# The z projections of a hybrid decoder step as block products with seven multiplications, two heads prepared in each

## Chip, cores and metric

One Trainium2 chip, one NeuronCore of it. The metric is the device time of one execution in microseconds; where several runs are given, their median.

## What is computed

One inference step of one decoder layer in float32, for 256 new tokens of a prompt and 8 x 4 tokens of running sequences: 288 token columns in all. Cut to what matters here:

```python
h = rmsnorm(x, norm1_w)
proj = jnp.einsum('btd,de->bte', h, w_in)      # 1024 -> pool 512, qkv 3072, a/b 16, z 1024, gates 2048
u_pool, u_qkv, b_raw, a_raw, z, gate_pool, gate_delta = jnp.split(proj, SPLITS, axis=-1)
y_pool, pool_buf_new = pool_mix(u_pool, pool_buf, ...)      # window means 2, 4, 8, 16, then w_pool
qkv, conv_buf_new = causal_conv(u_qkv, conv_buf, w_conv)    # width 4, then silu
o, s_new = gated_delta_chunked(l2norm(q), l2norm(k), v, g, beta, s0, chunk)   # 8 heads of 128
o = rmsnorm(o, o_norm_w) * jax.nn.silu(z)
merged = sigmoid(gate_pool) * (y_pool @ w_branch_pool) + sigmoid(gate_delta) * (o @ w_branch_delta)
x = x + merged @ w_out
x = x + hier_moe(rmsnorm(x, norm2_w), ...)     # 32 experts, top 2; gate, up, down
```

## The kernel before, in words

Each engine has its own program, written out by hand in order, and they meet at semaphores. There is no scheduler. The instructions of one engine run strictly in the order in which they stand.

**Projections.** `PROJ` lists 52 chunks of 128 output channels: 0 to 23 are q, k, v; 24 to 27 the pool groups; 28 to 35 z, a head each; 36 to 51 the gates. Two neighbouring chunks share one weight item of 1 MB (item 14 holds chunks 28 and 29). SyncE loads the items in order into slots of the arena (`SLOT_OF`), each when the item that held the slot has been read. Between the loads it issues the other transfers at fixed item numbers: `CONV_AT` and `ROWS_AT` (18), `CONV_AT + 1` (pool rows), `CONV_AT + 2` and `+ 3` (`load_states`), item 21 (a block of zeros from `X` to `x_image`), `DIAG_AT` (24).

**Two ways to multiply.** `proj(n)` makes one chunk with 8 matmuls of 288 columns. `fast_pair(i)` makes both chunks of an item by Strassen's scheme in Winograd's form: 7 block products P1, P6, P5, P7, P2, P3, P4 of 4 matmuls of 144 columns each. For it GpSimd makes four sums of weight blocks (`sum_weights`: four additions of 128 x 512) into slot 4 or 5. ScalarE copies P1 and P2 out of PSUM, and VectorE makes five additions of 144 columns (`add_u2`, `add_u4`, `add_u7`, `add_u5`, `add_u6`). P3 waits for `add_u4`, P4 for `add_u7`. Before, `FAST` holds items 1 to 11 (q, k, v) only.

**The stage of the change.** After q, k, v come the four pool chunks. VectorE makes the window sums of each group (`window(g)`, L2547 to L2558), TensorE then the four `pool_mix` products (L1564). Two z chunks are made among these (`Z_AHEAD`). After that comes a loop over the eight heads: `proj` of one more chunk, then `prep(h)` on TensorE (two products of keys with keys and queries, L1594). On VectorE `prep(h)` adds the decay rows to a mask (L2576), waits for ScalarE's three exponentials (`rows_exp`, L1067, L1070), multiplies (L2580) and scales the products (L2584, L2587). Between the heads stand small steps for the sample tokens (`sample_rows`, `sample_tiles`, `sample_flips`), and after head 4 `state_products(0)` (L1630). This one waits for `zb`, which GpSimd raises by `own_columns(0)` (L837), and `own_columns(0)` waits for the block of zeros to be in `x_image`. The decay rows of the heads go a round trip through DRAM (`head_rows`: out at L534, back to all partitions at L538). z itself leaves PSUM by a Silu on ScalarE (L975), one per chunk.

**Further on.** Gate chunks, the inversion of the 16 x 16 blocks (`diagonal_blocks` on SyncE, started when all eight heads are prepared), the scan over the chunks, the branches, `w_out`, and then the experts, whose weights (3 MB for each of 32) are streamed from DRAM.

The lines that bring the stage's order about:

```python
for n in range(Z_AHEAD):
    proj(N_Z + n)
    pool_mix(2 * n)
    pool_mix(2 * n + 1)
...
for h in range(H):
    proj(N_Z + Z_AHEAD + h)
    prep(h)
...
```

Of the kernel before, what the change touches and what calls it, by code (L numbers as in the profile page):

```python
# [21 lines left out]
H = 8  # L22
# [32 lines left out]
FAST = range(1, NQKV // 2)  # L55
# [4 lines left out]
SLOT_OF = [i % 4 if i < NQKV // 2 else i % RA for i in range(A_ITEMS)]  # L60
# [6 lines left out]
def sums_slot(i):  # L67
    return 4 + i % 2
# [21 lines left out]
Z_AHEAD = 2  # L90
# [12 lines left out]
MIX_BANK = (7, 4)  # L103
CONV_AT = NQKV // 2 + RA
ROWS_AT = NQKV // 2 + RA
DIAG_AT = (N_GATE + 2) // 2 + RA - 1
# [24 lines left out]
def hybrid_step(nc, x_prompt, x_sample, cache_pool, cache_conv, state_delta, norm1_w, w_in, w_pool,  # L131
# [24 lines left out]
    with ExitStack() as ctx:  # L156
# [288 lines left out]
        parts = zT.rearrange("p c t -> p (c t)")[:, 0:6 * HT].rearrange("p (j u t) -> p j u t", j=2, u=3)  # L445

# [32 lines left out]
        def _(sp):  # L479
# [29 lines left out]
            def store_conv():  # L509
# [10 lines left out]
                for b_ in range(BD):  # L520
                    store(new_conv_sample[0, b_], CW - 1 + 7 * b_ + TD)

# [8 lines left out]
            def head_rows():  # L531

                sp.wait_ge(S["row_ev"], 1)
                sp.dma_start(rows_image, by_row).then_inc(S["row_dma"], 16)  # L534
                sp.wait_ge(S["row_dma"], 16)
# [14 lines left out]
            for i in range(A_ITEMS):  # L550
# [37 lines left out]
                if i == ROWS_AT:  # L588
                    head_rows()
# [95 lines left out]
        def _(pool):  # L685
# [67 lines left out]
            def sum_weights(i):  # L753
# [5 lines left out]
                if i - 2 in FAST:  # L759
                    pool.wait_ge(S["proj"], product(i - 2, P4))  # L760
# [32 lines left out]
            for i in FAST:  # L793
# [3 lines left out]
                if i + 1 in FAST:  # L797
                    sum_weights(i + 1)
# [3 lines left out]
            for g in range(NG):  # L802
                if g >= 2:
# [4 lines left out]
                    pcT[:, g, :].rearrange("p (b r) -> p b r", b=BD)).then_inc(S["e_cache"], 1)  # L808

# [10 lines left out]

            pool.wait_ge(S["conv"], NQKV)
# [21 lines left out]
            nc.gpsimd.memset(XT, 0.0).then_inc(S["memsets"], 1)  # L843
            pool.wait_ge(S["diag"], 16)
# [65 lines left out]
        def _(act):  # L910
# [38 lines left out]
            def evac(n):  # L949
# [24 lines left out]
                elif n < N_GATE:  # L974
                    nc.scalar.activation(zT[:, n - N_Z, :], src[:, 0:T], ACT.Silu).then_inc(S["proj_free"], 1)  # L975
# [24 lines left out]
            def first_product(i):  # L1000

                act.wait_ge(S["proj"], product(i, P1))
                nc.scalar.activation(parts[:, i % 2, 0], ps[0][:, 0:HT], ACT.Copy).then_inc(S["proj_free"], 1)

            def first_tokens(i):
# [8 lines left out]
                nc.scalar.activation(E[n % 3][:, CW - 1:CW - 1 + HT], ps[0][:, 0:HT], ACT.Copy).then_inc(S["proj_free"], 1)  # L1014

# [15 lines left out]
            for i in FAST:  # L1031
# [50 lines left out]
            act.wait_ge(S["stage_out"], 16 * 2 * (1 + BD))  # L1082
            act.wait_ge(S["newp_t"], NG)
            nc.scalar.activation(stage[0:PBUF, 0:512], ps[2][0:PBUF, :], ACT.Copy).then_inc(S["newp_ev"], 1)
            nc.scalar.activation(stage[0:TS, 512:1024], ps[6][0:TS, :], ACT.Copy).then_inc(S["newp_ev"], 1)
            for n in range(Z_AHEAD):
                evac(N_Z + n)
                pool_rows(2 * n)
                pool_rows(2 * n + 1)
            for h in range(H):  # L1090
# [4 lines left out]
                evac(N_Z + Z_AHEAD + h)  # L1095
            evac(N_Z + Z_AHEAD + H)
            for n in range(N_GATE + 3, N_GATE + LEAD_GATES):
                evac(n)

# [275 lines left out]
        def _(pe):  # L1375
# [61 lines left out]
            def fast_pair(i, between):  # L1437

                w = slots[SLOT_OF[i]].rearrange("p (k n) -> p k n", k=KD)
# [11 lines left out]
                if i != FAST[0]:  # L1451
                    pe.wait_ge(S["sums"], added(i - 1, SUM5))
                else:
                    pe.wait_ge(S["small_ev"], 4)
                block_product(ps[4], s1, t1_)
                between()
                pe.wait_ge(S["pads"], weights_summed(i, 3))
                if i != FAST[0]:
# [1724 lines left out]
```

## Time and profile before

| | us |
|---|---|
| runs | 576.58, 578.35, 578.54 |
| median | 578.35 |
| profiled execution, its own time | 577.42 |
| its span, first to last instruction | 575.7 |
| TensorE busy | 537.8 (93%) |
| VectorE busy | 276.5 (48%) |
| ScalarE busy | 152.8 (27%) |
| GpSimd busy | 135.6 (24%) |
| mean granted TensorE clock | 0.982 of full speed |

The shares are means over stages with different limits: TensorE is busy nearly without a break in the first 340 us, and the transfers of the expert weights fill the DMA engines after that. What a change in one place is worth has to be read at that place.

### The profile page before, as it was taken

The numbers are of one execution on the slowest core, as the hardware profiler recorded it, in microseconds if no ns is written. First come the engines' busy times: TensorE is split into PE (matmuls) and PEld (weight loads), VectorE is DVE, ScalarE is ACT, GpSimd is POOL, SyncE is SP. The second block draws the span as 40 slices with busy tenths as digits, with TensorE's granted clock in tenths as the row PEclk, the third lists the DMA queues.
The fourth block names the chain that finished last, engine by engine and source line by source line (L and its number), as shares of the span: only waits on it lengthen the run. The fifth ranks groups of instructions, "written<-read, shape, count | busy, mean of one in ns | idle before, by whom it ended". The sixth has DMA issues, their size and how long they took to land. (4 is left out here: it accounts for less than half of the span.)

```text
span 575.7 us, 13023 instructions
## 1 busy us (share of the span) xinstructions
PE 537.8 (93%) x5284; PEld 409.5 (71%) x5284; DVE 276.5 (48%) x803; ACT 152.8 (27%) x408; POOL 135.6 (24%) x218
## 2 busy tenths in 40 slices
PE   7999999999999999999999999999999959699974
PEld 6899999877788776779899888656455535265432
DVE  2767668782532626335766244534524231405045
ACT  3258465316851012133200123210111101010105
POOL 6587677013020081033224132000000000000001
PEclk9999999999999999999999999999998989889998
DMA  9735444657984154745387898899999999999992
GB/s 275 220 112 158 129 160 148 211 174 276 313 233 161 12 159 163 221 142 151 109 274 299 350 425 299 344 408 422 397 422 420 421 418 421 422 418 420 405 374 93
DMA packets 81229, 158.02 MB, mean 274 GB/s; under 512 B 11166, under 2 KB 65067, under 8 KB 68979
## 3 DMA queue, kind: packets, MB, share of 16 engines
q1 hardware_dynamic: 78604, 153.69, 72.8%
q10 hardware_dynamic: 2567, 3.51, 2.0%
q8 instruction: 42, 0.69, 0.5%
q14 instruction: 16, 0.13, 0.1%
HBM read 149.40 MB, written 7.96 MB: 273 GB/s over the span
## 5 line engine op out<-in xcount | busy, mean ns | idle before, releaser
L1426 PE MATMUL ps<-arena 128*128 128x288 f32 x480 | 122.6, 410 | 0.9 <-DVE arena L2341 0.7
L1426 PEld LDWEIGHTS ps<-arena 128*128 128x128 f32 x480 | 89.4, 190 | 26.5 <-issue 2.3
L2090 PE MATMUL ps<-arena 128*32 128x256 f32 x1024 | 64.7, 411 | 15.2 <-DMA arena<-in_w_up_dram 13.6
L1433 PE MATMUL ps<-arena 128*128 128x144 f32 x616 | 78.3, 287 | 0.0
L1433 PEld LDWEIGHTS ps<-arena 128*128 128x128 f32 x616 | 76.3, 190 | 2.4 <-issue 1.9
L2090 PEld LDWEIGHTS ps<-arena 128*32 128x32 f32 x1024 | 37.8, 118 | 40.1 <-issue 24.6
L906 POOL TENSOR_TENSOR arena<-arena 128x512 f32<-128x512 f32 x2 | 2.5, 1274 | 207.2 <-ACT arena L1339 207.2
L2366 DVE SCALAR_TENSOR_TENSOR ps<-arena,ps 128x312 f32<-128x312 f32 x72 | 39.1, 544 | 2.2 <-ACT ps L1026 0.9
L1379 PE MATMUL ps<-arena 128*128 128x128 f32 (+7 forms) x162 | 26.7, 284 | 7.4 <-DVE arena L3052 5.1
L2005 PE MATMUL ps<-arena 128*128 128x128 f32 x256 | 32.3, 279 | 0.7 <-DVE arena L3030 0.6
L2005 PEld LDWEIGHTS ps<-arena 128*128 128x128 f32 x256 | 29.8, 192 | 3.6 <-issue 2.5
L1949 PE MATMUL ps<-arena 128*128 128x256 f32 x128 | 31.0, 385 | 0.0
L1379 PEld LDWEIGHTS ps<-arena 128*128 128x128 f32 (+7 forms) x162 | 18.9, 149 | 15.1 <-issue 6.4
L1901 PE MATMUL ps<-arena 128*128 128x144 f32 x224 | 27.9, 286 | 0.2 <-DVE arena L2870 0.2
L1901 PEld LDWEIGHTS ps<-arena 128*128 128x128 f32 x224 | 27.6, 190 | 0.6 <-DVE arena L2870 0.4
L3052 DVE TENSOR_TENSOR arena<-arena,ps 128x256 f32<-128x256 f32 x8 | 3.4, 421 | 50.0 <-issue 37.2
L2151 PE MATMUL ps<-arena 128*32 128x512 f32 x224 | 25.5, 595 | 0.5 <-ACT arena L1263 0.5
L3068 DVE TENSOR_TENSOR arena<-arena,ps 128x512 f32<-128x512 f32 (+1 forms) x35 | 21.6, 633 | 9.0 <-PE ps L2171 9.0
L1949 PEld LDWEIGHTS ps<-arena 128*128 128x128 f32 x128 | 23.1, 190 | 3.0 <-issue 0.4
L977 ACT ACTIVATE arena<-ps 128x288 f32<-128x288 f32 x16 | 6.6, 411 | 60.0 <-PE ps L1426 60.0
L3001 DVE COPY arena<-ps 128x512 f32<-128x512 f32 x8 | 5.5, 690 | 32.0 <-PE ps L2005 32.0
L3059 DVE COPY sc<-ps 128x512 f32<-128x512 f32 x7 | 4.8, 691 | 32.0 <-PE ps L2151 32.0
(438 smaller groups left out, 807.9 us busy)
## 6 DMA issues: line engine op xcount, KB each, us to landing
arena<-in_w_gate_dram SPq DMA_DIRECT2D x32, 1024.0 KB, 12.9
arena<-in_w_up_dram SPq DMA_DIRECT2D x32, 1024.0 KB, 16.6
arena<-in_w_down_dram SPq DMA_DIRECT2D x28, 1024.0 KB, 17.0
arena<-in_w_in_dram SPq DMA_DIRECT2D x26, 1024.0 KB, 5.7
out_dram<-arena SPq DMA_DIRECT2D x9, 512.0 KB, 7.2
arena<-in_w_branch_delta_dram SPq DMA_DIRECT2D x4, 1024.0 KB, 5.8
arena<-in_w_out_dram SPq DMA_DIRECT2D x4, 1024.0 KB, 5.2
arena<-in_state_delta_dram SPq DMA_DIRECT2D x7, 512.0 KB, 8.5
```

Of the source, the lines that this page charges most:

```text
L977: nc.scalar.activation(gT[:, n - N_GATE, :], src[:, 0:T], ACT.Tanh, scale=0.5).then_inc(S["proj_free"], 1)
L1379: return nc.tensor.transpose(out, in_, ident[0:m, 0:m])
L1426: last = mm(ps[n % 2][:, 0:T], w[:, k, P * (n % 2):P * (n % 2) + P], hT[:, k, :], start=(k == 0), stop=(k == KD - 1))
L1433: last = mm(to[:, 0:HT], left[:, k, :], right[:, k, :], start=(first and k == 0), stop=(k == HK - 1), skip_group_check=True)
L1901: last = mm(bank[:, 0:HT], left[:, k, :], right[:, k, :], start=(first and k == 0), stop=(k == HK - 1), skip_group_check=True)
L1949: last = mm(bank[:, 0:256], merged[:, k, P * t:P * t + P], w[:, k, :], start=(k == 0), stop=(k == KD - 1))
L2005: ins = mm(to, x2p[:, t, k, :], G[:, t, :], start=(first and k % 4 == 0), stop=(last_tile and k % 4 == 3), skip_group_check=True)
L2090: last = mm(to[CAP * e:CAP * e + CAP, 0:FE], xgT[:, k, CAP * e:CAP * e + CAP], w[e][:, k, :], start=(k == 0), stop=(k == KD - 1))
L2151: last = mm(ps[5 + half][CAP * e:CAP * e + CAP, :], actT[:, c, CAP * e:CAP * e + CAP], w[:, c, 512 * half:512 * half + 512], start=(c == 0 ...
L2366: ins = V.scalar_tensor_tensor(c, e[:, j:j + NACC], smallT[:, NQKV * j + n:NQKV * j + n + 1], c, ALU.mult, ALU.add)
L3001: V.tensor_copy(xgT[:, 0:4, :].rearrange("p k t -> p (k t)"), ps[0][:, :]).then_inc(S["m_xg0"], 1)
L3068: V.tensor_tensor(v, v, bank[:, 0:v.shape[1]], ALU.add).then_inc(S["m_yadd"], 1)
```

## The change

1. Items 14 to 17 (all of z) join `FAST`: each becomes a `fast_pair` with banks 3 and 4 for P5/P3 and P7/P4. GpSimd gets four more `sum_weights`: items 14 and 15 among the pool groups' copies, 16 before `row_masks`, 17 after the memset of `XT`.
2. `prep` of two heads goes with each of the pairs 15, 16 and 17: the first inside the pair (after P5), the second after it. Heads 6 and 7 go with the first two gate chunks. The four `pool_mix` go with pair 14.
3. z is put raw into `zT` and gets its Silu later, in three instructions among the gate chunks (`Z_SILU_AT`), with no Silu among the exponentials.
4. VectorE: `sample_quarters` (16 copies) moves from behind `window(1)` to between the additions of pair 14. `prep_rows(h)` is split off `prep(h)` and stands earlier.
5. Slots: items up to 17 use four slots instead of six, so that slots 4 and 5 hold sums. `CONV_AT` and `ROWS_AT` go from 18 to 16, the block of zeros from item 21 to 19, `DIAG_AT` from 24 to 23.
6. SyncE: the head rows go out ahead of the conv stores, and come back among them (after the third pair of stores). ScalarE: the copies of the pool rows (`newp_rows`) move from ahead of the first z chunk to behind the exponentials of head 0.

```diff
-FAST = range(1, NQKV // 2)
+QKV_FAST, Z_FAST = range(1, NQKV // 2), range(N_Z // 2, N_GATE // 2)
+FAST = (*QKV_FAST, *Z_FAST)
-SLOT_OF = [i % 4 if i < NQKV // 2 else i % RA for i in range(A_ITEMS)]
+SLOT_OF = [i % 4 if i < Z_FAST.stop else (2, 3, 0, 1, 4, 5)[i % RA] if i < Z_FAST.stop + RA else i % RA for i in range(A_ITEMS)]
-Z_AHEAD = 2
+Z_SILU_AT = {4: slice(0, 3), 6: slice(3, 6), 8: slice(6, H)}
-MIX_BANK = (7, 4)
-CONV_AT = NQKV // 2 + RA
-ROWS_AT = NQKV // 2 + RA
-DIAG_AT = (N_GATE + 2) // 2 + RA - 1
+MIX_BANK = (7, 5)
+CONV_AT = NQKV // 2 + 4
+ROWS_AT = NQKV // 2 + 4
+DIAG_AT = N_GATE // 2 + RA - 1
...
                 for b_ in range(BD):
                     store(new_conv_sample[0, b_], CW - 1 + 7 * b_ + TD)
+                    if b_ == 1:
+                        head_rows_back()
...
-                if i == RA + 15:
+                if i == RA + 13:
                     sp.wait_ge(S["memsets"], 1)
                     sp.dma_start(x_image, X[:, 0:2 * H * TILE]).then_inc(S["diag"], 16)
+                if i == ROWS_AT:
+                    head_rows_out()
...
                 nc.gpsimd.tensor_copy(
                     EP[g % 2][:, PE0:EPW].rearrange("p (b r) -> p b r", b=BD)[:, :, 0:PBUF],
                     pcT[:, g, :].rearrange("p (b r) -> p b r", b=BD)).then_inc(S["e_cache"], 1)
+                if g % 2 == 1:
+                    sum_weights(Z_FAST[g // 2])
...
+            sum_weights(Z_FAST[2])
             pool.wait_ge(S["conv"], NQKV)
             pool.wait_ge(S["wp_pe"], NG)
...
             row_masks()
             nc.gpsimd.memset(XT, 0.0).then_inc(S["memsets"], 1)
+            sum_weights(Z_FAST[3])
             pool.wait_ge(S["diag"], 16)
             own_columns(0)
...
+            first_product(Z_FAST[0])
+            pool_rows(0)
+            pool_rows(1)
+            z_first_tokens(Z_FAST[0])
+            pool_rows(2)
+            pool_rows(3)
+            for i in Z_FAST[1:]:
+                h = 2 * (i - Z_FAST[1])
+                first_product(i)
                 rows_exp(h)
-                if h == 1:
+                if h == 0:
+                    newp_rows()
+                z_first_tokens(i)
+                rows_exp(h + 1)
...
+            fast_pair(Z_FAST[0], first_mixes)
+            pool_mix(2)
+            pool_mix(3)
...
+            for i in Z_FAST[1:]:
+                h = 2 * (i - Z_FAST[1])
+                fast_pair(i, lambda: prep(h))
+                sample_step(h)
+                prep(h + 1)
+                sample_step(h + 1)
+            for n in range(2):
+                proj(N_GATE + n)
+                prep(H - 2 + n)
+            proj(N_GATE + 2)
             state_products(1)
...
+            add_u2(Z_FAST[0])
+            add_u4(Z_FAST[0])
+            sample_quarters((0, 1))
+            add_u7(Z_FAST[0])
+            sample_quarters((2, 3))
+            add_u5(Z_FAST[0])
+            add_u6(Z_FAST[0])
...
+            prep_rows(0)
+            for i in Z_FAST[1:]:
+                h = 2 * (i - Z_FAST[1])
+                add_u2(i)
+                add_u4(i)
+                prep(h)
+                add_u7(i)
+                prep_rows(h + 1)
+                if h >= 2:
+                    sample_step(h - 1)
+                add_u5(i)
+                add_u6(i)
+                sample_step(h)
+                prep(h + 1)
+                prep_rows(h + 2)
```

**TensorE, from the end of the pool chunks to the last `pool_mix`.** `L1426` and `L1469` are `proj`, `L1476` is a block product, `L1564` and `L1612` are `pool_mix`; `ps` numbers are banks. Before:

```order
L1426 MATMUL ps0<-arena 128x288 x8
L1564 MATMUL ps7<-arena 128x288
L1564 MATMUL ps4<-arena 128x288
L1426 MATMUL ps1<-arena 128x288 x8
L1564 MATMUL ps7<-arena 128x288
L1564 MATMUL ps4<-arena 128x288
```

With the change:

```order
L1476 MATMUL ps0<-arena 128x144 x4
L1476 MATMUL ps1<-arena 128x144 x4
L1476 MATMUL ps3<-arena 128x144 x4
L1612 MATMUL ps7<-arena 128x288
L1612 MATMUL ps5<-arena 128x288
L1476 MATMUL ps4<-arena 128x144 x4
L1476 MATMUL ps0<-arena 128x144 x4
L1476 MATMUL ps3<-arena 128x144 x4
L1476 MATMUL ps4<-arena 128x144 x4
L1612 MATMUL ps7<-arena 128x288
L1612 MATMUL ps5<-arena 128x288
```

Two products of 8 matmuls have become seven of 4 with half the columns; two of the mixes stand inside.

**VectorE, from `window(3)` to the first row of head 0.** `L2619` to `L2630` are the window, `L2447`, `L2453`, `L2460`, `L2469`, `L2478` the five additions, `L2571` and `L2573` `sample_quarters`, `L2652` `prep_rows(0)`. With the change (before, no addition stood here, and the copies ahead of `window(2)`):

```order
L2630 SCALAR_TENSOR_TENSOR arena<-arena 128x32
L2447 TENSOR_TENSOR arena<-arena,ps1 128x144
L2453 TENSOR_TENSOR arena<-arena,ps3 128x144
L2571 COPY sc<-sc 32x14
L2573 COPY arena<-U4 32x32
...
L2460 TENSOR_TENSOR arena<-arena,ps4 128x144
...
L2469 TENSOR_TENSOR arena<-arena,ps3 128x144
L2478 TENSOR_TENSOR arena<-arena,ps4 128x144
L2652 TENSOR_TENSOR arena<-arena 128x256
```

Eight copies stand between the second addition and the third, eight more ahead of the fourth.

**GpSimd, from the pool groups' copies to the memset of `XT`.** `L820` are the copies of the pool groups, `L775` to `L780` one `sum_weights`, `L845` `row_masks`, `L860` the memset. With the change (before, the three blocks of four additions were not there):

```order
L820 COPY arena<-arena 128x8x15 x2
L775 TENSOR_TENSOR arena<-arena 128x512
L777 TENSOR_TENSOR arena<-arena 128x512
L778 TENSOR_TENSOR arena<-arena 128x512
L780 TENSOR_TENSOR arena<-arena 128x512
L826 MEMSET arena 128x2048
L829 MEMSET arena 128x256
L831 AFFINE_SELECT arena<-arena 128x256
...
L845 TENSOR_TENSOR arena<-U4,sc 32x4x64
L845 TENSOR_TENSOR arena<-arena,sc 32x4x64 x2
L860 MEMSET arena 128x2048
```

The sums of item 15 stand right behind the last copies, where VectorE makes `window(2)` and `window(3)`; those of item 16 stand where "..." is, and those of item 17 behind the memset.

## Rows read from the trace of the kernel before

**Rows 1.** The page, the span in 40 slices: DMA share.

```profile
DMA  9735444657984154745387898899999999999992
```

**Rows 2.** Busy time in one stretch: us, PE, PEld, DVE, ACT, POOL, PEclk, DMA share, GB/s.

```profile
450.00:500.00 50.00, 39.28 (x452) 21.52 (x441) 17.05 (x47) 4.14 (x9) 0.00 (x0) 0.93 1.01 420
```

**Rows 3.** Timeline of PE: start, us, line, shape, count [idle before <-releaser].

```profile
93.96 7.03 PE L1433 MATMUL ps<-arena 128*128 128x144 f32 x56
100.83 0.27 PE L1379 MATMUL ps<-arena 128*118 128x128 f32 x1
...
125.24 4.05 PE L1426 MATMUL ps<-arena 128*128 128x288 f32 x16
129.13 1.13 PE L1564 MATMUL ps<-arena 128*128 128x288 f32 x4
...
161.04 3.70 PE L1630 MATMUL ps<-arena 128*32 128x128 f32 x128
164.67 4.15 PE L1426 MATMUL ps<-arena 128*128 128x288 f32 x16
168.65 1.03 PE L1594 MATMUL ps<-arena 128*128 128x256 f32 x4
```

**Rows 4.** Timeline of DVE, the copies and windows 2 and 3.

```profile
120.60 0.16 DVE L2501 COPY arena<-sb_small 32x8 f32<-32x8 f32 x1
120.79 1.89 DVE L2499 COPY sc<-sc 32x14 f32<-32x14 f32 x1
...
124.14 1.86 DVE L2547 TENSOR_TENSOR arena<-arena 128x422 f32<-128x422 f32 x3
...
127.12 2.48 DVE L2547 TENSOR_TENSOR arena<-arena 128x422 f32<-128x422 f32 x4
...
130.49 0.19 DVE L2558 SCALAR_TENSOR_TENSOR arena<-arena 128x32 f32<-128x32 f32 x1
```

**Rows 5.** Timeline of DVE, two additions beside GpSimd's later sums of weights.

```profile
297.57 0.46 DVE L2877 TENSOR_TENSOR arena<-arena 128x288 f32<-128x288 f32 x1
...
298.28 1.29 DVE L2874 SCALAR_TENSOR_TENSOR arena<-arena 128x288 f32<-128x288 f32 x1
299.61 1.41 DVE L2877 TENSOR_TENSOR arena<-arena 128x288 f32<-128x288 f32 x1
```

**Rows 6.** Timeline of POOL: the stage's memset, `own_columns(0)`, and the sums beside Rows 5.

```profile
120.85 1.80 POOL L810 MEMSET arena<- 128x2048 f32 x1
...
158.00 2.22 POOL L837 COPY arena<-arena 128x32 f32<-128x32 f32 x8 [19.11 <-DMA x_image<-arena]
...
297.98 1.27 POOL L865 TENSOR_TENSOR arena<-arena 128x512 f32<-128x512 f32 x1 [21.32 <-PE ps L1901]
299.33 1.36 POOL L867 TENSOR_TENSOR arena<-arena 128x512 f32<-128x512 f32 x1
```

**Rows 7.** Timeline of SP: DMA issues.

```profile
116.60 13.94 SPq L517 DMA_DIRECT2D out_dram<-arena  x18
...
133.63 2.52 SPq L526 DMA_DIRECT2D out_dram<-arena  x1
...
139.31 0.41 SPq L567 DMA_DIRECT2D arena<-in_w_in_dram  x1
...
150.30 1.80 SPq L583 DMA_DIRECT2D x_image<-arena  x1
```

**Rows 8.** Timeline of ACT: the first of two pool row copies, the first exponentials.

```profile
132.12 0.59 ACT L1084 ACTIVATE arena<-ps 15x512 f32<-15x512 f32 x1 [7.16 <-DMA out_dram<-arena]
...
135.77 1.28 ACT L1067 ACT_TABLE_LOAD   x1
139.72 0.31 ACT L1067 ACTIVATE arena<-arena 128x128 f32<-128x128 f32 x1 [2.67 <-DVE arena L2576]
139.93 0.68 ACT L1070 ACTIVATE arena<-arena,sc 128x128 f32<-128x128 f32 x2
```

**Rows 9.** The page's DMA issues: count, KB each, median us from issue to landing.

```profile
arena<-in_w_in_dram SPq DMA_DIRECT2D x26, 1024.0 KB, 5.7
```

More of the change, by code:

```diff
@@ L758, in sum_weights @@
                 pool.wait_ge(ring_in[SLOT_OF[i]], 16 * loads_in(SLOT_OF[i], i + 1))
-                if i - 2 in FAST:
-                    pool.wait_ge(S["proj"], product(i - 2, P4))
+                before = [j for j in FAST if j < i and sums_slot(j) == sums_slot(i)]
+                if before:
+                    pool.wait_ge(S["proj"], product(before[-1], P4))
                 nc.gpsimd.tensor_tensor(s1, a21, a22, ALU.add).then_inc(S["pads"], 1)
@@ L792, in _ @@
             old_columns(1)
-            for i in FAST:
+            for i in QKV_FAST:
                 raw_copy(2 * i - 2)
@@ L1014, in first_tokens, with z_first_tokens, z_silu @@
                 nc.scalar.activation(E[n % 3][:, CW - 1:CW - 1 + HT], ps[0][:, 0:HT], ACT.Copy).then_inc(S["proj_free"], 1)
+            def z_first_tokens(i):
+                act.wait_ge(S["proj"], product(i, P2))
+                nc.scalar.activation(zT[:, 2 * i - N_Z, 0:HT], ps[0][:, 0:HT], ACT.Copy).then_inc(S["proj_free"], 1)
+            def z_silu(chunks):
+                act.wait_ge(S["proj_free"], free[N_GATE - 1])
+                nc.scalar.activation(zT[:, chunks, :], zT[:, chunks, :], ACT.Silu).then_inc(S["wp_ev"], 1)
             def tap(n):
@@ L1030, in _ @@
             evac(1)
-            for i in FAST:
+            for i in QKV_FAST:
                 tap(2 * i - 2)
@@ L1437, in fast_pair @@
             def fast_pair(i, between):
+                third, fourth = pair_banks(i)
                 w = slots[SLOT_OF[i]].rearrange("p (k n) -> p k n", k=KD)
@@ L1464, in fast_pair @@
                 pe.wait_ge(S["sums"], added(i, SUM4))
-                block_product(ps[4], s4, b22, first=False)
+                block_product(third, s4, b22, first=False)
                 pe.wait_ge(S["sums"], added(i, SUM7))
-                block_product(ps[5], a22, t4_, first=False)
+                block_product(fourth, a22, t4_, first=False)
             def squares(j):
@@ L1581, in _, with first_mixes @@
             new_pool(NG - 1)
-            for n in range(Z_AHEAD):
-                proj(N_Z + n)
-                pool_mix(2 * n)
-                pool_mix(2 * n + 1)
+            def first_mixes():
+                pool_mix(0)
+                pool_mix(1)
+            fast_pair(Z_FAST[0], first_mixes)
+            pool_mix(2)
+            pool_mix(3)
             def prep(h):
@@ L1642, in sample_flips, with sample_step @@
                 last.then_inc(S["dec_pe"], 1)
-            pe.wait_ge(S["silu"], 3 * NQKV)
-            for h in range(H):
-                proj(N_Z + Z_AHEAD + h)
-                prep(h)
+            def sample_step(h):
                 if h == 0:
@@ L2382, in add_u2 @@
             def add_u2(i):
-                p1, u2, u4 = [parts[:, i % 2, j] for j in range(3)]
+                p1, u2, u4 = [pair_parts(i)[:, j] for j in range(3)]
                 dve.wait_ge(S["proj_free"], free[2 * i])
@@ L2501, in sample_quarters @@
                         link(V.tensor_copy(to[own, :], src))
-            for i in FAST:
+            for i in QKV_FAST:
                 if i != FAST[0]:
@@ L2661, in _, with sample_step @@
             dve.wait_ge(S["wp_pe"], NG)
-            for h in range(H):
-                prep(h)
+            def sample_step(h):
                 if h == 0:
```

105 lines of the change are left out of this document (65 added, 40 removed).

## The prediction, made before the change was run

> **What bounds the kernel now.** I read the slices of the page first, then one late stretch, then the timelines of the stage that the change touches, engine by engine. The slices show the DMA engines full (digit 9) from slice 26 on and with gaps before [rows 1]. In a late stretch TensorE is busy 39.28 of 50 us while 420 GB/s come in [rows 2]: there the stream of expert weights is the limit. Ahead of it TensorE is. In the timeline of TensorE around z, each group begins before the modelled end of the one before it, with no idle time noted [rows 3]. The loads of the expert weights wait for semaphores that TensorE's own stages raise (y_done, bd_pe, wo_pe, xp_pool in the code), so a microsecond that TensorE gains in the z stage moves the start of the stream, and the end, by about one microsecond. VectorE and ScalarE are half idle over the span, but that says nothing here: what counts is which of them is late when TensorE asks.
>
> **TensorE's own work.** A pair of chunks made by block products takes from 93.96 to 100.83, 6.87 us for 56 records [rows 3] (each matmul leaves two). A chunk made by `proj` takes from 125.24 to 129.13, 3.89 us, or after a row of small products 3.98 (164.67 to 168.65) [rows 3]. Eight chunks lie between 31.1 and 31.8 us; four pairs take 27.5. The change saves 3.6 to 4.3, and I take 3.8. The mixes, the preparations and the sample steps stay and only change places. The stage's last common point is `state_products(0)`: before it starts at 161.04 with seven z chunks done [rows 3]; with the change all eight are done there. Without a new wait it would start at nearly the same time, and the chunk at 164.67 would be gone. The gain is one chunk less whatever the start has slipped.
>
> **VectorE beside GpSimd: the main cost.** The trace shows what a sum of weights does to an addition with both inputs in SBUF. The addition L2877 of 288 columns takes 0.46 us alone; beside GpSimd's sums one takes 1.41 and L2874 of the same size 1.29, ending 0.3 us after GpSimd's current operation [rows 5, 6]. GpSimd's next sum then takes 1.36 instead of 1.27 [rows 6]. So they go one after the other, and each such addition is late by up to 0.95. This is what the change puts into the stage: three blocks of four sums, 5.1 us each (four of 1.27 [rows 6]), right where VectorE runs windows and preparations (the fourth block, item 14, lies earlier, beside window 0, where VectorE then waits for its inputs anyway).
>
> Pair 14: the sums of item 15 start at 120.9, behind GpSimd's last copy, about when window 2 can start (the small copies that delayed it before are moved away). Windows 2 and 3 are 6.5 us of VectorE (124.14 to 130.68 [rows 4]), nearly all with both inputs in SBUF. Now they can start 3.1 us earlier, at 121.0, and are held up by four sums, about 1.1 each with the 0.1 that overlaps: 121.0 + 6.5 + 4.4 = 131.9, less 0.5 that window 2's first operation and GpSimd's first sum share: 131.4. `add_u2` and `add_u4` (some 0.3 us each, as in the other pairs) follow. TensorE reaches P3 at 125.24 + 5 x 0.98 + 1.0 for two mixes = 131.1 and finds `add_u4` 0.6 us late, counted with the semaphores. Then VectorE makes eight copies, 0.2 us each by the start of two neighbours, 120.60 and 120.79 [rows 4], ahead of `add_u7`, which P4 waits for. One such copy took 1.89 beside GpSimd's memset of 1.80 [rows 4, 6], and a short memset and select of GpSimd fall here again: 2.1 to 2.3 us from `add_u4`'s end to `add_u7`'s, while TensorE has one block product of 0.98: 1.1 us late. Together 1.7; bounds 0 (the windows are not held up) and 3.5 (each of some eight operations late by 0.95 less the 3.1 that windows start earlier, plus the copies).
>
> Pair 16: `prep_rows(2)` and L2580 of head 2 stand beside the sums of item 17 and are late by up to 0.95 each, 1.9 in all [rows 5]. Behind them on VectorE is `add_u7`, and then the seven small operations of the sample mask, which TensorE's `sample_tiles` after the pair waits for. VectorE has almost no slack in this pair, so most of it arrives: I take 1.5, bounds 0 and 1.9. The sums of item 16 fall beside head 0; there the first exponential is late anyway and hides it.
>
> **A memset beside the windows.** GpSimd's memset of `X` (1.80 us [rows 6]) now follows the sums and lies beside window 3. No row shows an addition with two SBUF inputs beside a memset. The nearest row is the held-up copy, 1.7 us [rows 4]; additions are seen held up only beside operations that read [rows 5, 6], so I take 0 and keep 1.7 for the range. The Trainium skill ("SBUF — State Buffer", section "Who interferes with whom") says that a VectorE instruction with two SBUF inputs contends with a GpSimd instruction that reads SBUF and not with one that only writes it: by that rule the memset costs 0 and my sum stands; with the copy's row instead, the kernel comes out 1.1 us slower than before.
>
> **The zeros in `x_image` and the pool rows.** This wait is hidden before by a hair: the zeros are there at 158.0, `own_columns(0)` takes 2.22, to 160.2, and TensorE starts `state_products(0)` at 161.04 [rows 3, 6]. On SyncE the chain is: copies of the pool rows on ScalarE, nine stores (133.63 to 139.31), one item, four states, one item, the zeros (issued at 150.30) [rows 7]. The change puts ScalarE's two copies (the first at 132.12 [rows 8], about 1.1 us for both) behind head 0's exponentials. Pair 15 begins at 125.24 + 6.87 + 2.0 for four mixes + 1.7 of waits = 135.8, its first product is out at 137.3, then come a table load of 1.28 and 0.9 of exponentials [rows 8], and the copies end at 140.9 instead of 133.2. Everything behind them on SyncE, item 18 and the states included, goes 7 us later or less. The conv stores took 0.77 each (13.94 for 18 [rows 7]); with the round trip of the head rows among them the rows are back before 130, so the 2 MB that held up the first pool store (2.52 for one, against 3.1 for the other eight, up to 139.31 [rows 7]) are out of the way. Stores then take 3.5, and item 18 is issued at 144.4. From the item at 139.31 to the landed zeros at 158.0 it took 18.7 us, behind a queue that was full [rows 6, 7]. With an empty queue it is at least 5.7 for the item [rows 9] and 8.1 for the 3.4 MB behind it at 420 GB/s [rows 2], 13.8. I take the middle, 16.3: zeros at 160.7, `zb` at 162.9. With one chunk of 3.9 less behind this point and 0.6 gained in all, TensorE comes at 161.04 + 3.9 - 0.6 = 164.3. So no new wait in the forecast; bounds 0 and 3.1 (stores 5.6 from 140.9, transfers 18.7 and `own_columns(0)` 2.2 as before: 167.4).
>
> **Edits that cost nothing.** Three late Silus with two table loads each (about 3.6 us of ScalarE) fit into the 3.9 us of one gate chunk, since two banks alternate; if not, the next chunk waits under 1 us. Five additions and two PSUM copies a pair replace a Silu a chunk: VectorE has room outside pairs 14 and 16. Slots: item 18 lands near 150 and is read near 169; item 19 near 158, read 10 us later. Items 24 and 25 now come after the diagonal blocks' transfers, near 208, and are read after 225. The diagonal blocks start from head 7's preparation, which keeps its place before the six gate chunks, so their slack stays.
>
> **Sum.** 3.8 saved, less 1.7 and 1.5: 0.6 us gained. The profiled execution took 577.42 (span 575.7), so it would be 576.8. The median of the runs, 578.35, is 0.9 above it and another run 0.8 below; the mean of these four times is 577.7, and I put the forecast on that: 577.1.
>
> **Rivals.** (a) VectorE is held up less, or has the slack: the saving comes nearly whole. For it: the eleven pairs for q, k, v run at 6.87 with sums of weights beside them. Against it: there VectorE's operations take one input from PSUM, in windows and preparations both come from SBUF. The zeros' chain then takes up to 0.5 of it, and the gain is 3.3 to 3.8: about 574.2. (b) Slower: the zeros decide. With the nine stores at 5.7 us and 18.7 from item to zeros, `zb` comes at 167.4 and `state_products(0)` waits 3.1 us: 0.6 gained becomes 2.5 lost, 580.2. It decides from zeros landing later than 162.1; beyond that each us costs one. For it: the four states of 512 KB keep all 16 engines busy. Against: the queue is empty at 140 now. (c) The block products don't run at 6.87 with two heads' preparations between them, since VectorE's in-order stream meets TensorE's at five points a pair: each pair loses 0.5 to 1 us more and the kernel is 1.5 to 3 slower than the forecast, 579 to 580.
>
> **Chances.** Forecast (within 1.5 us of 577.1) 0.60, (a) 0.20, (b) 0.10, (c) 0.10. The range takes in (a) and (b): 574.2 to 580.2. About 0.5% of the time, 2.9 us, is what a measurement of this kernel can tell from no change. Faster by more than that needs (a) nearly whole: 0.17. Slower by more needs (b) or (c) at their ends: 0.11. Within 0.5%: 0.72.
>
> **What would show it.** In the profile after: pairs of 6.9 us; idle time of TensorE ahead of P3 and P4 of the first z pair (0.6 and 1.1, on `add_u4` and `add_u7`) and ahead of P4 and `sample_tiles` of the third, on VectorE; windows 2 and 3 stretched to some 10 us with additions above 1 us; `state_products(0)` between 164 and 166, released by TensorE's own order and not by `own_columns(0)`; and the same distance from there to the end, less one chunk. The prediction is wrong if the windows keep their 0.6 us an addition beside the sums, or if `state_products(0)` waits for the zeros, or if the distance behind it changes.

## The result: slower by 0.3%, the time inside the range and on the wrong side

| | before | after |
|---|---|---|
| median of 22 runs each, us | 577.61 (575.54 to 579.33) | 579.56 (576.27 to 582.68) |
| ratio to before, 95% interval | | 1.0029 (1.0015 to 1.0042) |
| profiled execution, its time / span, us | 577.42 / 575.7 | 579.49 / 577.8 |
| first pool chunk to `state_products(1)`, us | 76.27 | 78.23 |
| from there to the end of the span, us | 391.5 | 392.1 |

577.1 was forecast, 0.5 us gained; about 2 were lost. The kernel was measured two more times, beside new runs of the kernel before: 1.0005 (0.9986 to 1.0025, 10 runs) and 1.0029 (1.0015 to 1.0043, 9 runs). Over all three its 41 runs have a mean of 578.93; 69 runs of the kernel before, made beside the experiments, have 577.57. So the loss is nearer to 1.4 than to 2 us.

The stage's ends on TensorE, the first pool chunk and `state_products(1)`, in the timelines of the kernel before and after:

```profile
107.91 1.38 PE L1426 MATMUL ps<-arena 128*128 128x288 f32 x5
...
184.18 0.30 PE L1630 MATMUL ps<-late_room,arena 128*32 128x128 f32 x1
```

```profile
107.50 1.86 PE L1469 MATMUL ps<-arena 128*128 128x288 f32 x7
...
185.73 0.30 PE L1684 MATMUL ps<-late_room,arena 128*32 128x128 f32 x1
```

TensorE after, from pair 14 on (answers to [rows 3]; L1476 block products, L1612 mixes, L1648 preparations, L1672 sample tiles):

```profile
124.84 3.11 PE L1476 MATMUL ps<-arena 128*128 128x144 f32 x24
127.78 1.13 PE L1612 MATMUL ps<-arena 128*128 128x288 f32 x4
128.75 2.12 PE L1476 MATMUL ps<-arena 128*128 128x144 f32 x16
131.86 1.22 PE L1476 MATMUL ps<-arena 128*128 128x144 f32 x8 [0.99 <-DVE arena L2453]
133.82 1.92 PE L1476 MATMUL ps<-arena 128*128 128x144 f32 x8 [0.74 <-DVE arena L2460]
135.53 2.12 PE L1612 MATMUL ps<-arena 128*128 128x288 f32 x4
...
154.31 1.25 PE L1476 MATMUL ps<-arena 128*128 128x144 f32 x8 [0.24 <-DVE arena L2460]
156.32 0.33 PE L1672 MATMUL ps<-arena 32*32 32x32 f32 x16 [0.77 <-DVE arena L2689]
...
170.76 1.47 PE L1695 MATMUL ps<-arena 128*32 128x128 f32 x32
```

P2 could hand over to P3 at 130.71 (128.75 + 2 x 0.98), and P3 starts at 131.86: 1.15 late, on `add_u4` (L2453). P4 could follow at 132.84 and starts at 133.82: 0.98 late, on `add_u7` (L2460). In pair 16 P4 is 0.41 late and `sample_tiles` 1.03, on the last operation of the sample mask (L2689). These are the four waits that the prediction named, 3.57 us against 3.2.

What it did not name stands in the rows behind them: P4 takes 1.71 us to the mixes instead of 0.98, the two mixes 1.92 instead of 0.97. The busy time in stretches (us, PE, PEld, DVE, ACT, POOL, then the granted clock, DMA share, GB/s) shows why:

```profile
131.00:134.00 3.00, 1.40 (x9) 1.22 (x10) 2.55 (x13) 0.20 (x1) 0.82 (x2) 1.00 0.44 98
134.00:135.00 1.00, 1.00 (x6) 1.00 (x7) 0.84 (x5) 0.00 (x0) 0.00 (x0) 0.62 1.07 365
135.00:136.00 1.00, 1.00 (x5) 0.86 (x4) 0.87 (x4) 0.00 (x0) 0.12 (x1) 0.50 1.09 389
...
137.00:138.00 1.00, 1.00 (x6) 0.85 (x5) 0.14 (x1) 0.54 (x2) 0.92 (x2) 0.67 0.00 0
138.00:139.00 1.00, 1.00 (x10) 1.00 (x9) 0.79 (x1) 0.46 (x2) 1.00 (x2) 1.00 0.00 0
```

TensorE worked 1.40 of the three us from 131 to 134. Then the granted clock is down to 0.5, the 1.2 GHz level, and from 138 on 1.0 (2.4 GHz) again. It costs 1.8 us: 0.73 in P4, 0.95 in the mixes, 0.1 in pair 15. The balance of the stage: the two distances say 1.96 lost (78.23 - 76.27). Four waits make 3.57, the clock 1.8, `sample_flips` (L1695) is 0.39 longer than before; what is left, 3.8, is what the block products saved.

VectorE and GpSimd after, the windows (answers to [rows 4, 6]; L2619 the windows' additions, L775 to L780 the sums of item 15's weights, L826 the memset of `X`):

```profile
120.55 4.79 DVE L2619 TENSOR_TENSOR arena<-arena 128x422 f32<-128x422 f32 x3 [1.59 <-POOL arena L820]
125.36 1.12 DVE L2622 TENSOR_TENSOR arena<-arena,sb_small 128x8 f32<-128x8 f32 x1
...
127.40 2.48 DVE L2619 TENSOR_TENSOR arena<-arena 128x422 f32<-128x422 f32 x4
...
130.78 0.19 DVE L2630 SCALAR_TENSOR_TENSOR arena<-arena 128x32 f32<-128x32 f32 x1
```

```profile
120.46 1.26 POOL L775 TENSOR_TENSOR arena<-arena 128x512 f32<-128x512 f32 x1
121.80 1.51 POOL L777 TENSOR_TENSOR arena<-arena 128x512 f32<-128x512 f32 x1
...
124.85 1.62 POOL L780 TENSOR_TENSOR arena<-arena 128x512 f32<-128x512 f32 x1
126.41 1.80 POOL L826 MEMSET arena<- 128x2048 f32 x1
```

Three additions take 4.79 instead of 1.86 beside the sums. The four of window 3 take 2.48, as before; the first of them starts beside the memset (126.41 to 128.21).

### The profile page after: what moved, and what is told of

Its sections match the earlier page's. It is cut to its first block and busy times, and to the rows that moved or that the text cites. A ratio compares the mean times of both kernels' runs of the same rounds, so it can differ in the third digit from the quotient of the medians.

```text
span 577.8 us, 13270 instructions
## 1 busy us (share of the span) xinstructions
PE 538.2 (93%) x5380; PEld 414.6 (72%) x5380; DVE 288.0 (50%) x823; ACT 140.3 (24%) x400; POOL 158.0 (27%) x234
## 5 line engine op out<-in xcount | busy, mean ns | idle before, releaser
L1476 PE MATMUL ps<-arena 128*128 128x144 f32 x840 | 108.7, 289 | 2.0 <-DVE arena L2453 1.0
L1476 PEld LDWEIGHTS ps<-arena 128*128 128x128 f32 x840 | 105.6, 191 | 5.7 <-issue 3.0
L1469 PE MATMUL ps<-arena 128*128 128x288 f32 x352 | 89.7, 409 | 1.4 <-DVE arena L2402 0.7
L1469 PEld LDWEIGHTS ps<-arena 128*128 128x128 f32 x352 | 65.6, 190 | 19.5 <-issue 1.5
L924 POOL TENSOR_TENSOR arena<-arena 128x512 f32<-128x512 f32 x2 | 2.5, 1269 | 207.8 <-ACT arena L1382 207.8
L2066 PEld LDWEIGHTS ps<-arena 128*128 128x128 f32 x256 | 29.8, 192 | 3.6 <-issue 2.5
L1962 PE MATMUL ps<-arena 128*128 128x144 f32 x224 | 27.9, 286 | 0.2 <-DVE arena L2971 0.2
L1962 PEld LDWEIGHTS ps<-arena 128*128 128x128 f32 x224 | 27.6, 190 | 0.6 <-DVE arena L2971 0.4
L2010 PEld LDWEIGHTS ps<-arena 128*128 128x128 f32 x128 | 23.1, 190 | 3.0 <-issue 0.4
L775 POOL TENSOR_TENSOR arena<-arena 128x512 f32<-128x512 f32 x15 | 19.1, 1272 | 6.5 <-PE ps L1476 4.7
```

The costliest lines, as they stand in the source:

```text
L775: nc.gpsimd.tensor_tensor(s1, a21, a22, ALU.add).then_inc(S["pads"], 1)
L1469: last = mm(ps[n % 2][:, 0:T], w[:, k, P * (n % 2):P * (n % 2) + P], hT[:, k, :], start=(k == 0), stop=(k == KD - 1))
L1476: last = mm(to[:, 0:HT], left[:, k, :], right[:, k, :], start=(first and k == 0), stop=(k == HK - 1), skip_group_check=True)
L1962: last = mm(bank[:, 0:HT], left[:, k, :], right[:, k, :], start=(first and k == 0), stop=(k == HK - 1), skip_group_check=True)
L2010: last = mm(bank[:, 0:256], merged[:, k, P * t:P * t + P], w[:, k, :], start=(k == 0), stop=(k == KD - 1))
L2066: ins = mm(to, x2p[:, t, k, :], G[:, t, :], start=(first and k % 4 == 0), stop=(last_tile and k % 4 == 3), skip_group_check=True)
```

## The experiments

All ratios stand against runs of the kernel before on the same chip. Of every run the mean granted clock is known too; (1 - clock) x span is called the clock lost, in us. It is 10.9 in the kernel before (69 runs, standard error 0.1) and 12.1 in the changed one (41 runs, 0.2). It counts all stretches alike, also those where TensorE is not the limit, so it is not a loss of time as it stands. The experiments 1 to 4 ran on one chip, 5 to 8 on a second, 9 to 11 on a third; the kernel before loses 11.4, 10.7 and 10.5 on them.

**1. The sums of item 15 early.** On GpSimd, nothing else moved:

```
-                if g % 2 == 1:
-                    sum_weights(Z_FAST[g // 2])
+                if g == 1:
+                    sum_weights(Z_FAST[0])
+                    sum_weights(Z_FAST[1])
```

> GpSimd's sums of the weights of item 15 are issued right behind those of item 14, in the stretch 113 to 118 us where it is idle, so that none stands beside windows 2 and 3. My theory: both idle times of TensorE in pair 14 (1.15 us ahead of P3, 0.98 ahead of P4) hang on the windows' end, and the fall of the granted clock behind them (1.8 us) hangs on the idle times. All go: 3.9 us less than the changed kernel, a ratio to the kernel before of about 0.997, granted clock 1.0 from 134 to 138. Rival A (the eight copies hold add_u7 in any case): only P3's wait goes, ratio 1.001. Rival B (the clock falls at this place whatever TensorE did before, because of what stands there): the waits go, the clock stays at 0.5 there, ratio 0.9998. Rival C (the zeros' way through DRAM decides once TensorE is earlier): state_products(0) waits for own_columns(0) and 2 to 3 us of the gain are lost.

Measured: 576.0 us, ratio 0.9973 (0.9958 to 0.9989); the stage 74.47 us (107.23 to 181.70). TensorE from P1 to the mixes behind pair 14, with no wait noted and at full clock (the mixes at 127.5 and the next pair left out; the second group is still 0.3 longer than four products of 0.98):

```profile
124.56 3.11 PE L1477 MATMUL ps<-arena 128*128 128x144 f32 x24
...
128.48 4.40 PE L1477 MATMUL ps<-arena 128*128 128x144 f32 x32
132.71 1.13 PE L1613 MATMUL ps<-arena 128*128 128x288 f32 x4
```

My theory gave 0.997; rival A (the copies hold `add_u7` in any case) and rival C (the zeros bind) fall. On the clock this run does not decide between a fall that follows the waits and one that comes by chance.

**2. The sixteen small copies behind `add_u7`.**

```
-            sample_quarters((0, 1))
             add_u7(Z_FAST[0])
-            sample_quarters((2, 3))
+            sample_quarters((0, 1, 2, 3))
```

> All sixteen small copies of VectorE stand behind add_u7 of pair 14 and none ahead of it. My theory: the wait ahead of P4 (0.98) goes and that ahead of P3 (1.15) stays. On the clock the theories part. If two waits close together are needed, it stays at 1.0: 2.8 us less than the changed kernel, ratio 0.998. If one wait of 1.15 us is enough, or the place alone, it falls all the same: 1.0 us less, ratio 1.0012. Rival (the copies were hidden): ratio stays 1.003.

Measured: 581.61 us, ratio 1.0065 (1.0044 to 1.0086). All that was expected of the time failed. P4's wait is gone, and a new one of 2.7 us stands ahead of P5 of pair 15, on `add_u5`. VectorE and GpSimd there:

```profile
134.07 1.25 DVE L2573 COPY arena<-sb_small 32x8 f32<-32x8 f32 x1
135.36 0.17 DVE L2571 COPY sc<-sc 32x14 f32<-32x14 f32 x1
135.56 1.14 DVE L2573 COPY arena<-U 32x32 f32<-32x32 f32 x1
...
137.95 1.18 DVE L2573 COPY arena<-sb_small 32x8 f32<-32x8 f32 x1
139.16 0.30 DVE L2469 TENSOR_TENSOR arena<-arena,ps 128x144 f32<-128x144 f32 x1
```

```profile
134.03 1.26 POOL L775 TENSOR_TENSOR arena<-arena 128x512 f32<-128x512 f32 x1 [2.22 <-PE ps L1476]
135.38 1.28 POOL L777 TENSOR_TENSOR arena<-arena 128x512 f32<-128x512 f32 x1
...
137.84 1.25 POOL L780 TENSOR_TENSOR arena<-arena 128x512 f32<-128x512 f32 x1
```

P4 earlier lets GpSimd start the sums of item 16 earlier, and they now meet the last copies: 1.14 to 1.25 us for a copy of 0.17. The page "SBUF — State Buffer" of the Trainium skill ("Who interferes with whom") names copies among the operations that can take the port pair which VectorE shares with GpSimd, and says that whichever engine is first then blocks the other; the rows agree, with GpSimd first. The clock did not fall here, behind waits of 1.0 and 2.7 us, so a fall does not come in every execution.

**3 and 7. TensorE kept busy in its waits.** In pair 14, ahead of each of the two waits (eight and six products of ones by the identity; in the second run four and three; the edit at the first wait is shown):

```
+                if i == Z_FAST[0]:
+                    pe.wait_ge(S["wp_ev"], 2)
+                    warm(8)
                 pe.wait_ge(S["pads"], weights_summed(i, 4))
                 pe.wait_ge(S["sums"], added(i, SUM4))
```

> The changed kernel with nothing moved, but TensorE multiplies ones by the identity into an idle bank while it waits: eight matmuls of 128 columns ahead of P3 of pair 14 and six ahead of P4. The waits themselves end when VectorE's sums are there, as before. My theory (idle time of TensorE brings the clock down): the clock stays at 1.0, P4 takes 0.98 instead of 1.7 and the two mixes 0.97 instead of 1.9, 1.8 us less than the changed kernel, ratio 1.000. Rival (the clock falls for another reason): no gain, ratio 1.003, or 0.2 to 0.4 slower where the fillers outlast the waits.

> As the experiment with fillers, but four ahead of P3 and three ahead of P4 of pair 14, since each took 0.23 to 0.25 us and eight and six outlasted the waits by 0.6 each. The fillers end before the waits do, so the stage itself neither gains nor loses, except by the clock. If idle TensorE costs clock, the mean granted clock rises from 0.978 to 0.980 and the time falls by 1 us, ratio 1.001. If not, ratio 1.003 and clock 0.978.

Measured: 581.68 us, 1.0075 (1.0054 to 1.0096), and 582.68 us, 1.0093 (1.0069 to 1.0117), both slower than every theory said. With the few fillers the stretch they were put in is right: no wait of TensorE shown, P3 and P4 where they were, clock 1.0. The loss is some 90 us further on, in code that the edit does not touch. TensorE, and a stretch behind it (columns as above):

```profile
218.49 0.66 PE L1769 MATMUL ps<-arena 32*32 32x32 f32 x54 [1.16 <-issue]
...
224.91 5.46 PE L1469 MATMUL ps<-arena 128*128 128x288 f32 x15 [3.57 <-issue]
```

```profile
225.00:228.00 3.00, 3.00 (x7) 2.12 (x7) 1.35 (x2) 0.00 (x0) 0.00 (x0) 0.50 0.03 9
```

TensorE stands 1.16 and 3.57 us in the middle of a group, waiting for nothing that the profile shows, and then the clock is 0.5. With the many fillers it is 0.74 and 3.08, and the clock 0.54. In the other eleven profiles such pauses of 0.4 to 1.4 stand near there. They lie where the DMA engines are full (share 1.03 to 1.12 from 210 to 222 us with the few fillers), and the long one ends about where that load does. The likeliest reason is the supply of instructions, which arrive by DMA queues of their own ("q8 instruction" and "q14 instruction" on the page) and whose places shift with the added instructions; that was only argued. As a test of what fillers do to the time the two runs are spoiled. What they do show is a second place where a fall of the clock follows a standstill of TensorE. In pair 14 neither has a fall, which decides nothing, since other kernels with the waits have none either.

**4. The sample tiles later.** On TensorE, `sample_tiles(2)` behind `prep(3)`, and `sample_tiles(3)` behind `prep(4)` within pair 17:

```
             for i in Z_FAST[1:]:
                 h = 2 * (i - Z_FAST[1])
-                fast_pair(i, lambda: prep(h))
-                sample_step(h)
+                if h < 4:
+                    fast_pair(i, lambda: prep(h))
+                else:
+                    def between():
+                        prep(h)
+                        sample_step(h - 1)
+                    fast_pair(i, between)
+                if h != 2:
+                    sample_step(h)
                 prep(h + 1)
-                sample_step(h + 1)
+                sample_step(h if h == 2 else h + 1)
```

> On TensorE alone: the tiles of the inverse's first step (sample_tiles 2) stand behind prep(3) instead of ahead of it, the second's stand after prep(4) within pair 17. My theory: the 1.03 us that TensorE waits for sample_masked in pair 16 is covered by prep(3)'s matmuls (1.1 us), and VectorE has room to take the tiles later: 0.8 to 1.0 us less than the changed kernel, ratio 1.0013. Rival: VectorE, which works without a gap from 151 to 164, takes inverse(0) and prep(3) a microsecond later and the wait reappears in pair 17: ratio 1.003.

Measured: 577.69 us, ratio 1.0000 (0.998 to 1.002), the expected 1.0013 inside the interval, whose width does not tell the wait's 1 us from nothing; the trace does. In pair 16 the preparation follows P4 and the tiles follow the preparation without an idle time:

```profile
151.99 1.25 PE L1476 MATMUL ps<-arena 128*128 128x144 f32 x8 [0.25 <-DVE arena L2467]
153.07 1.03 PE L1648 MATMUL ps<-arena 128*128 128x256 f32 x4
154.03 0.33 PE L1672 MATMUL ps<-arena 32*32 32x32 f32 x16
```

The rival (the wait comes back in pair 17) falls. Pair 14's waits are as in the changed kernel (0.99 and 0.73 shown), and this execution had no fall of the clock behind them either.

**5 and 10. The waits put back by themselves.** To experiment 1 were added ten and twenty copies of 32x32 on VectorE ahead of `add_u2` of pair 14:

```
+            for _ in range(10):
+                link(V.tensor_copy(strict4[0:TS, :], S4[:, :]))
             add_u2(Z_FAST[0])
```

> The kernel of sum15_early, in which TensorE had no wait in pair 14, with ten small copies of VectorE (0.2 us each by the trace) put ahead of add_u2 of pair 14: both waits of TensorE are back, about 1.1 us ahead of P3 and 1.0 ahead of P4, and no sum of weights stands beside the windows. If the windows' lateness alone makes the loss, the stage takes 2.1 us more than that of sum15_early and the ratio to the kernel before goes from 0.997 to 1.001. If such waits also bring the clock down in part of the executions, the mean granted clock falls from 0.981 to about 0.978 and the ratio comes to 1.003, as in the changed kernel. Rival (it was GpSimd's sums beside VectorE that cost something of their own): ratio stays near 0.998.

> As the experiment that put ten small copies of VectorE back ahead of add_u2 (waits of 1.54 and 0.51 us), but with twenty: the wait ahead of P3 grows by 2.0 us to about 3.6, that ahead of P4 stays. By the waits alone: 2.0 us more than with ten, 580.9, ratio 1.0055. If the chance of a fall of the clock grows with the time that TensorE stands still, the mean clock goes to 0.976 and the ratio to 1.007 to 1.008. Rival (TensorE has slack of some 2 us further on that takes up a late pair 14): ratio stays near 1.002.

Measured: with ten 578.83 us, ratio 1.0018 (1.0000 to 1.0035); with twenty 582.12 us, 1.0079 (1.0064 to 1.0094). In the three kernels the waits shown are 0, 2.05 and 3.57 us, the ratios 0.9973, 1.0018 and 1.0079. (With twenty, the wait ahead of P4 is gone, against the expectation.) The first ratio lies between the two that were expected, 1.001 and 1.003, and its interval holds both. Lateness of VectorE at this point is enough to make the loss, and nothing here shows that GpSimd's sums beside the windows cost more than that lateness. By the ratios the ten copies cost 2.6 us (interval some 1.4 either way) for 2.05 of waits, ten more 3.5 (1.3) for 1.5; only the second step is clearly larger than the waits it adds. The clock lost grows: against the kernel before on the same chip it is 0.6 less in experiment 1, 1.7 more with ten and 2.7 more with twenty (12, 12 and 5 runs, standard errors 0.45, 0.3 and 0.6). Both profiles show the fall behind the waits; the one with ten copies, then with twenty:

```profile
131.00:134.00 3.00, 1.22 (x8) 1.03 (x8) 2.51 (x14) 0.06 (x1) 0.00 (x0) 0.98 0.20 58
134.00:138.00 4.00, 4.00 (x15) 3.61 (x16) 1.94 (x10) 0.64 (x2) 1.48 (x2) 0.59 0.87 267
```

```profile
132.00:135.60 3.60, 0.03 (x1) 0.03 (x1) 2.98 (x18) 0.29 (x1) 0.00 (x0) 0.98 0.26 57
135.60:139.00 3.40, 3.40 (x15) 3.40 (x16) 2.86 (x17) 0.00 (x0) 0.00 (x0) 0.52 0.91 302
```

**6 and 9. The changed kernel again.**

> The changed kernel as it is, for a second profile of it. In its first one the granted clock fell to 0.5 from 134 to 138 us, behind two waits of TensorE; in two experiments with the same waits or longer ones it did not. If the fall belongs to the waits, it is here again at the same place. If it comes in some executions and not in others, it is absent here or elsewhere, and the stage from the first pool chunk to state_products(1) takes 76.4 instead of 78.2 us.

> The changed kernel once more, against new runs of the kernel before, for the size of the loss (1.0029 in its first measurement, 1.0005 in the second, whose interval reaches from 0.9986 to 1.0025) and for a third profile. If the loss is about 1.3 us, the mean of both, the ratio comes to 1.002. If a fall of the clock behind pair 14's waits comes in some 7 of 10 executions, as the mean granted clocks suggest (1.2 us of clock lost more than in the kernels without the waits, 1.7 us for one fall), the mean clock is again about 0.979 and this profile shows it more likely than not.

Measured: 578.08 us, 1.0005 (0.9986 to 1.0025), and 578.52 us, 1.0029 (1.0015 to 1.0043). Both profiles have the four waits as in the first and neither has the fall; the second (start, us, as above, and a stretch):

```profile
131.08 1.22 PE L1476 MATMUL ps<-arena 128*128 128x144 f32 x8 [0.99 <-DVE arena L2453]
133.04 1.25 PE L1476 MATMUL ps<-arena 128*128 128x144 f32 x8 [0.74 <-DVE arena L2460]
134.12 1.13 PE L1612 MATMUL ps<-arena 128*128 128x288 f32 x4
```

```profile
134.00:138.00 4.00, 4.00 (x31) 3.79 (x30) 1.89 (x7) 2.68 (x5) 3.48 (x3) 1.00 0.42 146
```

So the fall comes in some executions of one and the same program. The stage took 76.38 us in the second (106.72 to 183.10), 0.1 from the 76.27 of the kernel before: at full clock and with no pause, four pairs and their waits cost what eight chunks cost. It took 77.81 in the first, where `sample_flips` was held 1.3 us by a pause that the profile lays to nothing (0.93 of it marked "issue").

**8 and 11. What the experiments point to.** Edits 1 and 4 together, in one run with the zeros' store (`x_image`) two items earlier on SyncE's queue:

```
-                if i == RA + 13:
+                if i == RA + 11:
                     sp.wait_ge(S["memsets"], 1)
```

> Three edits together: the sums of item 15 early, the tiles of the first two inverse steps later on TensorE, and the store of the zeros (x_image) right behind item 17 on SyncE's queue instead of item 19. My theory: the waits of pair 14 (2.1 us) and of sample_tiles 2 (1.0) go, and with the store early own_columns(0) follows the sums of item 17 on GpSimd, so it does not bind: stage 73.5 us, ratio to the kernel before 0.9955. Rival (the zeros' copies or VectorE's chain behind the later tiles hold state_products(0)): ratio 0.9973 as with the first edit alone.

> The experiment with three edits less one: the zeros' store stays behind item 19. In the trace of sum15_early own_columns(0) ended at 161.3 us; state_products(0) stood at 161.6 with all three edits. If that margin of 0.3 us holds, the early store was worth nothing and the ratio is 0.995 again, own_columns(0) about 12 us later than with it. Rival (the zeros decide by now): state_products(0) waits 0.5 to 2 us, ratio 0.996 to 0.998.

Measured: 574.39 us, ratio 0.9950 (0.9934 to 0.9966), with all three; 575.23 us, 0.9958 (0.9944 to 0.9971), without the store's move. Both beat both kernels. GpSimd's `own_columns(0)` in the two traces, three moves first, and TensorE's start of `state_products(0)` in the second:

```profile
147.19 2.38 POOL L855 COPY arena<-arena 128x32 f32<-128x32 f32 x8
```

```profile
158.83 2.28 POOL L855 COPY arena<-arena 128x32 f32<-128x32 f32 x8 [11.64 <-DMA x_image<-arena]
```

```profile
161.55 3.70 PE L1685 MATMUL ps<-arena 128*32 128x128 f32 x128
```

More than eleven us earlier, and the intervals of the two overlap; the stage takes 73.66 and 73.64 us. The store's place is worth nothing that was measured, though only 0.4 us lie between the end of `own_columns(0)` at 161.1 and TensorE at 161.55.

## Why the prediction was wrong

- **TensorE's own work: right to 0.3.** 3.8 taken. The balance of the first profile leaves 3.8, that of the third 3.5 (3.57 of waits, and 0.1 lost, with no fall of the clock and no pause). Pair 15 takes 7.2 us there and its P4 is 0.3 late on `add_u7`; pair 14 of experiment 1 takes 7.2 with its two mixes taken off (132.71 - 124.56 - 0.97); pairs of q, k, v 6.87. This is rival (c), at about a third of its size.
- **Pair 14: mechanism right, 0.4 short.** Windows 2 and 3 ran from 120.55 to 130.97, 10.4 us, as forecast. P4 was 0.98 late (1.1 forecast), P3 1.15 (0.6). Here the text's own terms were added wrongly: windows' end at 131.4, plus 0.6 for two additions, against TensorE at 131.1, makes 0.9 before any semaphore. The upper bound of 3.5 does not come out of its terms either: eight times 0.95, less 3.1, is 4.5 before the copies.
- **Pair 16: right.** 1.44 us against 1.5, at the two places named; L2580's and `prep_rows(2)`'s operations take 1.16 instead of 0.29 and 1.49 instead of 0.42 beside the sums of item 17. Experiment 4 took the larger wait away by order alone: TensorE had independent work of 1.03 us (`prep(3)`) behind the wait.
- **The memset: right.** Price 0. The rule of the Trainium skill cited there ("SBUF — State Buffer", "Who interferes with whom") agrees with the rows: an addition of window 3 beside the memset keeps its 0.62. The copy's row, the other bound, was another case (a copy and not an addition).
- **The zeros: right that they do not bind, with luck.** They landed at 162.85, 2.1 later than forecast and later than the 162.1 from which the text had them decide. `own_columns(0)` ended at 165.2; it did not bind because TensorE was late too, `state_products(0)` starting at 166.07 (164.3 forecast), in its order.
- **The sum failed.** "3.8 saved, less 1.7 and 1.5: 0.6 us gained" is at full clock 3.5 less 2.13 and 1.44: 0.1 lost, as the third profile has it. Of the rest of the loss (1.4 us by the means, 1.95 by the medians of the first measurement) the traces show two parts that the sum had no term for. The step that failed is the price of a wait: it was put at its own length, with nothing for the clock that can fall behind it. That fall cost 1.8 us in the first of the three profiles of the changed kernel and is absent in the other two. The second part is the time that `sample_flips` stands still: 0.39, 1.3 and 0 us in the three, 0 in the one of the kernel before. Over the three the stage takes 77.5 us in the mean against 76.27; about half of the difference is the one fall and about half the pauses, but three executions give no more than the order of size.
- **How much of the mean loss is clock stays open.** The changed kernel has 1.2 us more of clock lost than the kernel before (standard error 0.25), but these are not 1.2 us of time. In the trace of before all of the clock lost lies behind 420 us, where the stream of weights is the limit (stretches as above: TensorE's busy time first, the granted clock and the DMA share near the end):

```profile
0.00:420.00 420.00, 410.76 (x3794) 335.91 (x3795) 227.15 (x668) 131.87 (x356) 133.08 (x216) 1.00 0.69 234
420.00:571.00 151.00, 127.00 (x1492) 73.55 (x1490) 48.88 (x134) 20.86 (x53) 2.51 (x2) 0.94 0.95 388
```

Over the 69 runs of the kernel before, the time does not go with the clock lost at all (0.06 us for each, standard error 0.14, within each chip); over the 41 of the changed kernel it goes by 0.5 (0.15).

- **Does the fall belong to the waits?** For it: of seven profiles with waits of 1 us or more in pair 14 or right behind it three show it, always behind them; of four without waits there (before, experiments 1, 8, 11) none. All five falls ahead of 420 us in the thirteen profiles stand behind a standstill of TensorE. On the same chip, kernels with the waits lose 0.9 us more of clock than the variants without them (standard error 0.3). Against its being a fixed price: four profiles have such waits and no fall, and three of seven against none of four can be chance. And experiment 8, which has no such waits, loses as much clock as the changed kernel beside it (11.5 and 11.3). So the link is likely and not shown. What decides in one execution stays open, and so does why the pauses marked "issue" come and go.
- The trace of before could have told. Its own expert stages show the price, in the timeline and in the stretches: TensorE waits 5.31 us for a weight, the clock is 0.62 in the mean of the next 7, and a group of 3.66 takes 6.07.

```profile
462.34 3.66 PE L2090 MATMUL ps<-arena 128*32 128x256 f32 x64 [0.86 <-issue]
471.31 6.07 PE L2090 MATMUL ps<-arena 128*32 128x256 f32 x64 [5.31 <-DMA arena<-in_w_up_dram]
```

```profile
471.00:478.00 7.00, 6.07 (x64) 3.09 (x64) 0.42 (x1) 0.00 (x0) 0.00 (x0) 0.62 1.02 424
```

There the kernel waits for memory anyway, so I had read it as harmless; the same row applied to 2 us of new waits in a stage that TensorE bounds would have given a rival of some 2 us (6.07 less 3.66 is 2.4). Rival (b) did not occur, (c) only in part, and (a) needed an order of GpSimd's work that the change did not have.

## What to carry to other kernels

When a change puts a new wait of TensorE into a stage that TensorE bounds, price the work behind it at both levels of the clock, with a chance, and not the wait alone. When VectorE shares a stretch with GpSimd, look first for an idle stretch of GpSimd earlier on: the same four sums cost TensorE no wait in pair 14 when they ran from 113 to 118 us, where VectorE had slack, and held up windows by 3.9 us from 120.5 to 126.4. An added instruction is no neutral probe: compare the trace also where nothing was edited. And the mean clock of a whole run is no measure of time: look in which stretch it was lost, and what is the limit there.

## What was not expected of the hardware

- The granted clock can fall to 0.5 (here from 134 to 138 us) behind TensorE's waits of 1.15 and 0.98 us that lie 2 us apart, and it can fail to in the next execution of the same program. One such fall costs 1.8 us.
- A one-input copy of 32x8 or 32x32 in SBUF takes 1.14 to 1.25 us instead of 0.17 beside GpSimd's sums, while additions with one input in PSUM keep their 0.30.
- Seven added products of TensorE went with 4.7 us of pauses some 90 us later (1.16 and 3.57), where 0.4 and 0.7 stood in the first profile of the changed kernel, and 2.1 in all at most in the others without added products.
